# The lone latent columns of `z` and `h` start at column 96 of their rows in place of 112 (two hybrid RG-LRU and MLP layers, one core)

## What is computed

```
def swiglu(z, w_in, w_out):
    gate, up = jnp.split(z @ w_in, 2, axis=-1)
    return (jax.nn.silu(gate) * up) @ w_out
...
    h = h + 0.5 * m[8] * swiglu(modulate(rmsnorm(h, ffn2_norm_g[l]), m[6], m[7]),
                                ffn2_w_in[l], ffn2_w_out[l])
    if not last:
        hc = hc + 0.5 * mc[8] * swiglu(...)
return rmsnorm(h, final_norm_g)
```

## The kernel before

| read by TensorE | starts at, modulo 512 bytes |
|---|---|
| a weight block of `w_hi` or `w_lo` | 128 |
| `z` or `h`, full row or `COLS[0]` or `COLS[1]` | 128 |
| `z` or `h` at `LAT0` = 112 (448 bytes on) | 64 |
| `y_hi_alone`, `y_lo_alone` | 64 |

## Time and profile before

### The profile page before, as it was taken

One profiled execution on the slowest core, in us unless ns is written; L12 is line 12 of the kernel. 1 busy time (PEld: TensorE's weight loads), 2 busy tenths in 40 slices (PEclk: granted clock), 3 DMA queues, 4 the chain that ended last, 5 costly groups with the idle time before them and its releaser, 6 DMA issues.

```text
span 1588.9 us, 22168 instructions
## 1 busy us (share of the span) xinstructions
PE 1563.4 (98%) x8994; PEld 1333.0 (84%) x8994; DVE 997.8 (63%) x1231; ACT 623.5 (39%) x840; POOL 89.7 (6%) x108
## 2 busy tenths in 40 slices
PE   7999999999999999999999999999999999899997
PEld 5888888888878888888888898888888897899997
DVE  6777773783867577677363267767455268865554
ACT  4433322232674353333232252333232259554453
POOL 0000000011100200000000100000001010100001
PEclk9999999999999999999999999999999999999999
DMA  9565553652422256565363336656354333446563
GB/s 362 190 194 186 179 166 119 204 193 82 131 67 80 93 161 194 179 196 172 106 199 100 99 120 212 197 177 196 93 185 129 97 103 123 143 161 194 191 205 113
DMA packets 72297, 249.94 MB, mean 157 GB/s; under 512 B 11664, under 2 KB 12816, under 8 KB 71184
## 3 DMA queue, kind: packets, MB, share of 16 engines
q1 hardware_dynamic: 72208, 248.70, 48.5%
HBM read 247.62 MB, written 1.05 MB: 157 GB/s over the span
## 4 chain that ended last, share of the span: by engine, by line
PE 94%; DVE 2%; ACT 1%; issue 1%; DMA 1%; SPq 0%; POOL 0%; DVEq 0%; POOLq 0%; ACTq 0%
PE bank L393 83%; PE bank L512 2%; PE bank L518 2%; PE bank L514 2%; PE bank L668 1%; DMA ada_head<-head_w 1%; PE bank L408 1%; PE bank L645 1%; PE bank L647 1%; PE bank L646 1%; PE bank L474 0%; DVE w_lo L1024 0%; PE bank L424 0%; ACT w_hi L783 0%; DVE l_q L1269 0%
## 5 line engine op out<-in xcount | busy, mean ns | idle before, releaser
L783 ACT ACTIVATE w_hi<-raw 128x1024 fp32r<-128x1024 f32 x320 | 339.3, 1060 | 823.1 <-PE bank L393 803.4
L1024 DVE TENSOR_TENSOR w_lo<-raw,w_hi 128x1024 fp32r<-128x1024 f32 x320 | 391.8, 1225 | 381.3 <-ACT w_hi L783 380.8
L393 PE MATMUL bank<-z_hi,w_hi 128*128 128x512 f32 (+1 forms) x1480 | 537.4, 363 | 0.3 <-DVE scr L1210 0.3
L393 PE MATMUL bank<-z_lo,w_hi 128*128 128x512 f32 (+1 forms) x1480 | 532.1, 360 | 0.0
L393 PE MATMUL bank<-z_hi,w_lo 128*128 128x512 f32 (+1 forms) x1480 | 532.0, 359 | 0.0
L393 PEld LDWEIGHTS bank<-z_hi,w_hi 128*128 128x128 f32 x1480 | 278.1, 188 | 47.2 <-issue 4.1
L393 PEld LDWEIGHTS bank<-z_lo,w_hi 128*128 128x128 f32 x1480 | 278.1, 188 | 43.5 <-issue 1.9
L393 PEld LDWEIGHTS bank<-z_hi,w_lo 128*128 128x128 f32 x1480 | 278.0, 188 | 42.6
L393 PE MATMUL bank<-h_hi,w_hi 128*128 128x512 f32 (+1 forms) x770 | 266.5, 346 | 0.0
L393 PE MATMUL bank<-h_lo,w_hi 128*128 128x512 f32 (+1 forms) x770 | 265.7, 345 | 0.0
L393 PE MATMUL bank<-h_hi,w_lo 128*128 128x512 f32 (+1 forms) x770 | 265.6, 345 | 0.0
(11 more groups left out here) (148 smaller groups left out, 1199.2 us busy)
## 6 DMA issues: line engine op xcount, KB each, us to landing
raw<-weights SPq DMA_DIRECT2D x320, 512.0 KB, 4.2
ada_raw<-ada_w SPq DMA_DIRECT2D x128, 512.0 KB, 4.3
ada_head<-head_w SPq DMA_DIRECT2D x8, 1024.0 KB, 18.6
res<-x_t SPq DMA_DIRECT2D x4, 512.0 KB, 5.8
bd<-gate_w SPq DMA_DIRECT2D x4, 256.0 KB, 5.5
out<-res SPq DMA_DIRECT2D x4, 256.0 KB, 3.1
ws<-sgu_w SPq DMA_DIRECT2D x2, 256.0 KB, 5.7
bs<-sgu_b SPq DMA_DIRECT2D x2, 256.0 KB, 5.2
```

The costliest lines, as they stand in the source:

```text
L393: m = pe.matmul(bank[:, to], w[:, r, c], x[:, k, at], start=start and i == 0, stop=stop and i == 2, skip_group_check=True)
L783: act.activation(w_hi[:, r, :], raw[:, r, :], ACT.Copy).then_inc(hi_ready, 1)
L1024: dve.tensor_tensor(w_lo[:, r, :], raw[:, r, :], w_hi[:, r, :].bitcast(F32), ALU.subtract).then_inc(lo_ready, 1)
```

## The change

One constant. `LAT0` goes from 112 to 96, so that the lone latent columns of `z_hi`, `z_lo`, `h_hi` and `h_lo` start 64 bytes earlier:

```
@@ -51,7 +51,7 @@
 WARM_UP = 8
 HEAD_AHEAD = 3
 ADA_RING = 2
-LAT0 = 112
+LAT0 = 96
 Y_ORDER = [(0, 1, 2, 3, 4, 5, 6, 7), (0, 1, 2, 4, 5, 6, 7, 3)]
```

## The result

| | before | `LAT0` = 96 |
|---|---|---|
| median | 1591.38 us (1588.67 to 1597.40, 15 runs) | 1598.59 us (1597.63 to 1600.43, 15 runs) |
| profiled execution | 1590.65 us, span 1588.9 | 1598.15 us, span 1596.4 |

The ratio is 1.0039 (95% interval 1.0028 to 1.0051): the change makes the kernel slower by 0.39%. The times of before fall in two groups: 11 of the 15 lie between 1588.7 and 1591.9 us, 4 between 1595.4 and 1597.4. The 15 of the changed kernel form one group. Against the lower group of before, median 1590.5 us, it is 8.1 us slower.

The account below looks back on a forecast made before the run. TensorE's matmul spacing was taken to bound the last FFN. From the profiled 1590.65 us, 0 for the dense matmuls and 0.2 off those ahead gave 1590.4 us, with an 8-in-10 range of 1588.5 to 1601.5.

Parts of the forecast that it names:

- What bounds the kernel: Last FFN: lasts as long as its matmuls from start to start; VectorE and ScalarE have 25 us of slack in 66.
- The first part: 30 writes on ScalarE and 30 on VectorE go 64 bytes lower, taken to cost nothing.
- the second: Dense piece of the last FFN: 1488 matmuls stay at 113.3 ns each, so no change.
- the picture of eight places of 64 bytes: Weight and moving reads wanting the same of eight places cost 16 cycles, once per matmul, twice when starting at the same place.
- The third part: 96 matmuls ahead of the dense piece go from 117.8 to 113.3 ns; 0 to 0.43 us gained, 0.2 taken.
- Back to 120 ns: Last FFN's matmuls cost 120 ns because the start leaves 64 modulo 128 bytes: 1600.8 us, chance 0.22.
- its rule of 128 bytes: Starts at 64 modulo 128 bytes cost 113.3 ns, starts at 0 modulo 128 cost 120 ns.
- Caught at 117.8: Dense piece falls into the other steady spacing, 117.8 ns, and keeps it: 1597.3 us; chance 0.12, including a mixture of spacings.
- No excess: Reads two pieces apart may not meet; last FFN's matmuls at 106.7 ns: 1579.7 us, chance 0.12 including part of it.
- the constant does nothing: The address doesn't matter, something else sets the spacings: 1590.65 us, sharing the 0.54 for same spacing or no effect.
- The bounds of that term: Price of each of the 1488 dense matmuls: at most 120 ns, at least 106.7 ns, that is 256 cycles without excess.

Follow-up runs that it names:

- the run with the weights at 384: Kernel with `LAT0` = 96, unused columns moving `w_hi` and `w_lo` to start at 384 modulo 512 bytes instead of 128: 1599.14 us, ratio 1.0052.
- 48: Kernel before with `LAT0` = 48 in place of 112, nothing else changed: 1590.58 us, ratio 0.9995.
- 80: Kernel before with `LAT0` = 80 in place of 112, nothing else changed: 1597.26 us, ratio 1.0029.
- 144: Kernel before with `LAT0` = 144 in place of 112, nothing else changed: 1597.63 us, ratio 1.0032.
- the kernel with the weights at 256: Kernel before with `LAT0` = 80 and unused columns moving `w_hi` and `w_lo` to start at 256 modulo 512 bytes: 1618.52 us, ratio 1.0171.

## Why the prediction was wrong

**What bounds the kernel** held. The piece that I named, the dense matmuls from the wait on, carries the whole difference, and slack on VectorE and ScalarE stayed slack: DVE is busy for 39.70 and ACT for 33.03 us in 66.00.

**The first part**, the 60 writes at no cost, is in keeping with the result: the chain from 1406.47 to 1409.76 us is as long as in the earlier trace rows.

**The step that failed is the second**, the price of the 1488 matmuls at a distance that no row had. It measured 118.7 ns, which over 1488 matmuls is the 7.9 us. I chose 113.3 ns, by the picture of eight places of 64 bytes where a meeting is paid once wherever one starts, except at distance 0. Three of its parts are wrong. The period is 256 bytes: the run with the weights at 384 and the pairs 48 and 112, 80 and 144 show it. And the excess is not once everywhere: at 256 columns it is 16 cycles or 26.7 at 64 bytes on either side, 28.8 or 32 at 128, 32 at 0. Nor is it the same at both widths, as the picture had it: at 512 columns it goes from 32 cycles at 0 to 48 at -64. What the picture had right is that the distance counts, in excesses of 16 cycles.

**The third part**, 0.2 us off the first four slots, went the other way and was small: these 96 are at 118.7 ns too, 0.1 us more. The 117.8 ns that I started from was itself one of two spacings there, as the further executions of the kernel before show.

**The rivals.** "Back to 120 ns" had the right direction, 1600.8 us against 1598.59, and the wrong reason; its rule of 128 bytes is refuted by 80, which it would have made fast. "Caught at 117.8" had 1597.3 us. It came near (1598.59) and its mechanism is real, but it describes what happens at 112, not at 96, which has 118.7 ns in every traced stretch. "No excess" and "the constant does nothing" fell. The 109.2 ns beside "no excess" come from a formula that the Trainium skill, "TensorE: Matmul & The Clock Gate", section "Back-to-back issue gap", gives for an isolated matmul, not for a stream of weight loads and matmuls as here. No run here shows them. What I should have weighed more: the rows had three prices for three situations, and a new distance is as likely to bring a new price as an old one. The bounds of that term, 106.7 and 120 ns, held, and so did the range.

**The two groups of before** I did not foresee, though the earlier trace rows have both spacings. My predicted 1590.4 us is the lower group. Over all comparisons 67 of 92 executions of the kernel before were in the lower (1588.7 to 1592.0 us), 25 in the upper (1595.4 to 1599.0).

**Open.** Why the excess has the size it has at each distance, and why 256 and 512 columns want opposite distances: the runs give the prices, not the mechanism. In particular, that the two reads meet somewhere in SBUF is my picture; the runs show only that the price goes with their distance. That the upper group of the kernel before itself is the dense piece at 117.8 ns is inferred from the kernel with the weights at 256; no upper execution of before was traced. What decides which group an execution falls in is open as well, and so is whether the dense piece at 96 ever takes the 120.0 ns that other stretches at this distance show; that would add 2.0 us to the traced 1598.15 (1488 x 1.33 ns), and the highest of its 15 times, 1600.43 us, leaves room for it.

## What to carry to other kernels

When TensorE streams fp32r and is never idle, the start of the moving columns and the start of the weight blocks are a tuning parameter together: here the price repeated every 256 bytes of their difference, and a constant 64 bytes off cost 5% of a stage in which nothing else changed. Measure the start-to-start spacing in the dense stretch, separately for each width, before moving anything: what was best for 256 columns was worst for 512. And look at all executions, not at the median alone; two groups of times can be two spacings of the same instructions, though the traces here show that for a sister kernel and for short stretches of this one, not yet for the upper group itself.

## What the hardware showed that I had not expected

- fp32r matmuls of 128 by 128 with a weight load each, at 2.4 GHz, by distance (start to start): 256 columns 120.0 ns at 0, 118.7 or 120.0 at 128, 113.3 or 117.8 at 64 on either side; 512 columns 226.7 ns at 0, 229.0 at +64, 232.4 or 233.3 at 128, 233.3 at -64. At 1.2 GHz the nine matmuls of the earlier trace rows have none of the excess.
- One instruction sequence at one address has two steady spacings (113.3 and 117.8 ns in the first slots of three executions of one kernel), and a dense piece keeps the one that it falls into: at distance -64 the 1488 matmuls are at 117.8 ns in one trace and at 113.3 in the others without interruptions.
- "SBUF — State Buffer" in the Trainium skill, section "Who interferes with whom", has TensorE's two read ports independent and TensorE waiting on no one. These runs disagree: moving only the weight blocks by 64 bytes, with no other engine's work changed, took the last FFN from 113.3 to 118.7 ns a matmul and the full rows from 226.7 to 233.3.
